# The low parts of the seven operand forms, made by GpSimd in place of VectorE

## The chip, the core and the metric

One core of a Trainium2 chip runs the whole program. A core has five engines that run their own instruction lists and meet at semaphores: TensorE (PE, with its weight loads shown as PEld), VectorE (DVE), ScalarE (ACT), GpSimd (POOL) and SyncE (SP, which here only starts DMAs). The metric is the device time of one execution in microseconds (us). The kernel before was timed three times: 2039.69, 2042.03 and 2042.06, median 2042.03.

## The reference

One decoder layer on 512 tokens of width 2048 in float32: an adaptive modulation, a mixer made of a gated recurrence and an attention with a forget bias, and an MLP with squared ReLU. The change lies in the MLP alone:

```python
def rms_norm(x, g):
    xf = x.astype(jnp.float32)
    y = xf * lax.rsqrt(jnp.mean(jnp.square(xf), axis=-1, keepdims=True) + EPS)
    return (y * g.astype(jnp.float32)).astype(x.dtype)
...
        x = x + gt1[:, None, :] * rms_norm(y, g_post_mix[l])
        h = modulate(rms_norm(x, g_pre_mlp[l]), sh2, sc2)
        y = jnp.square(jax.nn.relu(h @ w_ff1[l])) @ w_ff2[l]
        x = x + gt2[:, None, :] * rms_norm(y, g_post_mlp[l])
```

`w_ff1` is 2048 x 8192 and `w_ff2` is 8192 x 2048.

## The kernel before

**Arithmetic.** Every float32 operand of a matmul is split in two parts of the type fp32r: a high part, which ACT makes by a copy that rounds, and a low part, the float32 value less the high part, which DVE makes. A product takes three matmuls: high by low, low by high, high by high. Both MLP products use a scheme with seven half-size products in place of eight (named P1, P5, P6, P3, P7, P2, P4 in the order of work), whose operands are sums of quadrants.

**The first MLP product (stage A).** The 8192 hidden columns are cut into 32 blocks of 256 (`b`). The first four are made in the usual way. For the other 28, each block is seven units on PE (`first_product`, L1142 to L1144), one for each of the seven products, and a unit is 8 x 3 matmuls of 128x256. For each unit the weight tile, or a sum of quadrants of it that DVE makes (`total`, L2210), is split: `high` on ACT (L1602), `low` on DVE (L2161). Three of the seven results stay in a bank that is read by ACT (`copy_sum`, L1579) and three are added by DVE to what was copied (`add_sum`, L2218). PE may not start P4 of a block until DVE has added P7, since both use one bank; nor P6 until ACT has copied P1.

**Closing a block.** When P4 of a block is done, ACT applies the ReLU (`rectify`, L1552 and L1554) and the square (`square_u`, L1560), which gives four quadrants of `u_forms`. DVE makes four sums of them (`operand_sums`, L2139 to L2144). Slots 1 to 7 of `u_forms` are then the seven forms, 128x1792. ACT copies them rounded to `hi_stage` (`operand_high`, L1573), DVE subtracts in place (`operand_low`, L2150), and GpSimd, whose list in this stage is nothing else, stores both parts to a scratch in HBM (`store_forms`, L2510 and L2512). Each store waits for its own part. The next block's `rectify` and `operand_high` wait until both stores of the block before have landed (`stored_through`), since there is one `u_forms` and one `hi_stage`.

**What sets the order.** The order on each engine is written out by hand. DVE and ACT run one loop over the units: at PE's unit n, DVE makes the low part of unit n + 2, adds or reads the result of unit n - 1, and makes the sum for unit n + 4; ACT makes the high part of unit n + 3. `CLOSE_AT[b]` gives the unit at which a block is closed: `rectify` there, the sums one unit on, `operand_high` two, `operand_low` three. For most blocks that is the first unit of the next block; blocks 4 and 5 are closed one unit later, and the last block (31) three units after stage A has ended.

**The second MLP product (stage B).** SP loads the stored forms into `op`, 1 MB at a time, and the `w_ff2` tiles; PE runs 16 groups of seven products (L1160 to L1162), DVE makes weight sums and low parts and reads the products out of PSUM (`read_product`, L2235 and L2237). P7 of a group may start only when DVE has read P6.

Of the kernel before, what the change touches and what calls it, by code (L numbers as in the profile page):

```python
# [16 lines left out]
F32 = mybir.dt.float32  # L17
F32R = mybir.dt.float32r
ALU = mybir.AluOpType
# [13 lines left out]
def hybrid_layer(nc, x, c, w_ada, b_ada, g_pre_mix, g_post_mix, g_pre_mlp, g_post_mlp, w_in, conv_w, conv_b,  # L33
# [24 lines left out]
    for which, (_, j0, j1) in enumerate(PASSES):  # L58
        for j in range(j0, j1):
            if which:  # L60
                BACK_UNIT[j] = len(FIRST_UNITS)
                FIRST_UNITS.append((which, j - j0))
            P_UNIT[j] = len(FIRST_UNITS)
            FIRST_UNITS.append((which, j))
            Q_UNIT[j] = len(FIRST_UNITS)
            FIRST_UNITS.append((None, j))
    assert len(BACK_UNIT) == 6
    DONE_PAIRS = {gi: j1 for gi, _, j1 in PASSES if gi is not None}
    V_FROM = [DONE_PAIRS.get(gi, 0) for gi in range(8)]
    START = [8 * gi - sum(V_FROM[:gi]) for gi in range(9)]  # L70
# [41 lines left out]
    BLOCKS = D_FF // 256  # L112
    FIRST = 4
    U_A = U_MLP + CONV
# [17 lines left out]
    def a_unit(n):  # L132

        return divmod(n - U_A, 7)
# [14 lines left out]
    def made_of_sums(n):  # L149

        if n >= U_END:
            return False
        if n < U_B:
            return 1 <= a_unit(n)[1] <= 4
        return b_unit(n)[1] in SUM_INDEX
# [44 lines left out]
    with ExitStack() as ctx:  # L200
# [3 lines left out]
        def sem(name):  # L204
            return ctx.enter_context(nc.semaphore(name))

        def overlay(*specs):

            with ExitStack() as phase:
                return [phase.enter_context(nc.sbuf_tensor(n, s, d)) for n, s, d in specs]  # L210
# [27 lines left out]
            ("h_hi", [P, KT, COLS], F32R), ("x_tok", [P, NT, D], F32), ("gst0", [P, 8, 2, 256], F32),  # L238
            ("xnT", [P, KT, COLS], F32), ("gst1", [P, 8, 2, 256], F32), ("junk", [P, D], F32))
        _, h_lo, hs, rg, ig, ut, wrg, wig, a_sq, sq = overlay(  # L240
            ("pad2", [P, KT, COLS], F32), ("h_lo", [P, KT, COLS], F32R), ("hs", [P, CT, COLS], F32),
            ("rg", [P, CT, COLS], F32), ("ig", [P, CT, COLS], F32), ("ut", [P, CT, COLS], F32),
# [16 lines left out]
        _, T34, u_forms, ext, T12, hsO = overlay(  # L259
            ("pad5", [P, 32 * 256], F32), ("T34", [P, 8, 2, 2, 256], F32R), ("u_forms", [P, 8, 256], F32), ("ext", [P, 4 * COLS], F32),  # L260
            ("T12", [P, 8, 2, 2, 256], F32R), ("hsO", [P, 2, 8, 2, 256], F32R))
# [40 lines left out]
        def stage_of(b):  # L302

            if b >= 3:
                return hi_stage[:, :, :]
            place_ = rows_base[:, :, :].rearrange("p a (s n) -> p (a s) n", n=256) if b == 0 else k_tile[2]
            return place_[:, 0:7, :].bitcast(F32R)
# [46 lines left out]
        with ExitStack() as whole:  # L354
# [66 lines left out]
        relu_done, u_done, u_sum, op_hi_ready, op_lo_ready = (  # L421
            sem(n) for n in ("relu_done", "u_done", "u_sum", "op_hi_ready", "op_lo_ready"))
# [1278 lines left out]
        def _(dve):  # L1701
# [433 lines left out]
            def operand_sums(b):  # L2135

                dve.wait_ge(u_done, b + 1)
                F = u_forms
                dve.tensor_tensor(F[:, 4, :], F[:, 0, :], F[:, 2, :], ALU.add).then_inc(u_sum, 1)  # L2139
                dve.tensor_tensor(F[:, 7, :], F[:, 1, :], F[:, 0, :], ALU.subtract).then_inc(u_sum, 1)  # L2140
                dve.wait_ge(u_sum, 4 * b + 1)
                dve.tensor_tensor(F[:, 5, :], F[:, 4, :], F[:, 1, :], ALU.subtract).then_inc(u_sum, 1)
                dve.wait_ge(u_sum, 4 * b + 3)
                dve.tensor_tensor(F[:, 6, :], F[:, 3, :], F[:, 5, :], ALU.subtract).then_inc(u_sum, 1)  # L2144

            def operand_low(b):

                dve.wait_ge(op_hi_ready, b + 1)
                F = u_forms[:, 1:8, :]
                dve.tensor_tensor(F.bitcast(F32R), F, stage_of(b).bitcast(F32), ALU.subtract).then_inc(op_lo_ready, 1)  # L2150

            def low(n):

                if n < U_A:
                    return lo_part(n)
                dve.wait_ge(hi_ready, n + 1)
                if n < U_B:
                    out_, w, hi = by_tile(w_lo, n), a_source(n), by_tile(w_hi, n)
                else:
                    out_, w, hi = w_lo[:, n % RING, :], b_source(n), w_hi[:, n % RING, :]  # L2160
                dve.tensor_tensor(out_, w, hi.bitcast(F32), ALU.subtract).then_inc(lo_ready, 1)  # L2161
# [50 lines left out]
            def add_sum(n):  # L2212

                blk, pos = a_unit(n)
                dve.wait_ge(unit_used, n + 1)
                dve.wait_ge(c_copied, 3 * blk + {P3: 3, P7: 2, P2: 1}[pos])
                s = c_sums[:, blk % 2, {P3: 0, P7: 2, P2: 1}[pos], :]
                dve.tensor_tensor(s, s, a_bank(blk, pos), ALU.add).then_inc(c_added, 1)  # L2218
# [3 lines left out]
            def read_product(m):  # L2222

                g, i = divmod(m, 7)
                kind = KINDS[g][i]
                K, r = divmod(g, 2)
                dve.wait_ge(unit_used, U_B + 2 * m + 2)
                if m:
                    dve.wait_ge(y_read, reads_before(m))
                targets = [(1, 0)] * ((g, kind) == (GROUPS - 1, P7)) + [TARGETS[kind]]  # L2230
                for th, side in targets:
                    y = y2[:, 2 * th:2 * th + 2, y_cols(0, side, r)]
                    bank = pairs_of(g, kind)[:, :, :]
                    if K == 0 and kind in (P1, P5, P6, P4):
                        ins = dve.tensor_copy(y, bank)  # L2235
                    else:
                        ins = dve.tensor_tensor(y, y, bank, ALU.add)  # L2237
                    ins.then_inc(y_read, 1)
# [60 lines left out]
            def gate_first(t):  # L2299
                dve.wait_ge(f_ssq, t + 1)  # L2300
                if t == 0:
                    dve.wait_ge(g2_in, 16)
                y = tile_cols(y2[:, t, :], 0)
                gated_at[t, 0] = gate_piece(y, y, None)

            def gate_inside(t, side, square):
                dve.wait_ge(f_ssq, square)
                cols = y_cols(t, side, 1)
                gated_at[t, 1] = gate_piece(y2[:, t, cols], y2[:, t, cols], cols)

            for n in range(U_A, U_END):
                if n + 2 < U_END:
                    low(n + 2)
                if U_A < n <= U_B and a_unit(n - 1)[1] in (P3, P7, P2):
                    add_sum(n - 1)
                if n > U_B and (n - U_B) % 2 == 0:
                    read_product((n - U_B) // 2 - 1)
                if made_of_sums(n + 4):
                    total(n + 4)
                for b, at in CLOSE_AT.items():  # L2320
                    if n - U_A == at + 1:
                        operand_sums(b)
                    elif n - U_A == at + 3:
                        operand_low(b)
                tail = n - G_LAST
                for t in {3: [0], 4: [1], 5: [2, 3]}.get(tail, []):
                    gate_first(t)
                if tail in (6, 11):
                    for t in range(2):
                        gate_inside(t, 0 if tail == 6 else 1, (5 if tail == 6 else 7) + t)  # L2330
# [46 lines left out]
        def _(pool):  # L2377
# [128 lines left out]
            def store_forms(b):  # L2506

                K, i = divmod(b, 4)
                pool.wait_ge(op_hi_ready, b + 1)
                pool.dma_start(u_scr[K, :, :, 0, i, :], stage_of(b).bitcast(F32)).then_inc(u_stored[b % 2], 16)  # L2510
                pool.wait_ge(op_lo_ready, b + 1)
                pool.dma_start(u_scr[K, :, :, 1, i, :], u_forms[:, 1:8, :]).then_inc(u_stored[b % 2], 16)  # L2512

            for b in range(BLOCKS):
                store_forms(b)
            pool.wait_ge(gate_stored, 16 * 8)
            pool.wait_ge(unit_used, U_B)
# [33 lines left out]
```

## Time and profile before

| | |
|---|---|
| median of three runs | 2042.03 us |
| the profiled execution | 2040.41 us, span 2038.6 us |
| PE busy | 1995.0 us, 98% of the span |
| DVE busy | 1739.0 us, 85% |
| ACT busy | 950.7 us, 47% |
| POOL busy | 141.7 us, 7% |
| granted PE clock | 0.993 of full |

The profiled execution's own time is 1.8 us over its span, for what lies before the first and behind the last instruction. Busy shares are means over the whole program. PE is the engine to look at first, and for the others the question at each place is how long before PE needs it their work is done. Stage A of the 28 blocks runs from about 839 us to 1410 us, stage B from there to the end.

### The profile page before, as it was taken

To read this page: it belongs to the slowest core of one execution; us is meant where nothing else is said; L and a number is where in the kernel's file an instruction comes from. 1 tells how busy PE (TensorE), PEld (TensorE's weight loads), DVE (VectorE), ACT (ScalarE), POOL (GpSimd) and SP (SyncE) were. 2 spreads that over 40 slices of the span, in tenths; PEclk is the share of its full clock that TensorE was granted. 3 is DMA by queue.
4 is the path that set the end of the run, shared out by engine and by line. 5 is a ranking of instruction groups with operands and counts; after the bars stand their busy time and mean duration, and the time that the engine had idled before them with its cause. 6 is when DMAs were issued, how large, how long until landed. Compare 5 with 4: busy or idle time off the path is not lost.

```text
span 2038.6 us, 28073 instructions
## 1 busy us (share of the span) xinstructions
PE 1995.0 (98%) x11091; PEld 1727.8 (85%) x11091; DVE 1739.0 (85%) x2010; ACT 950.7 (47%) x1208; POOL 141.7 (7%) x160
## 2 busy tenths in 40 slices
PE   7999999999999989999999999999999999999996
PEld 5887788888778878899999999999888888888885
DVE  7999897786987888788888888888988888888889
ACT  6434632224553267565656555555333333333343
POOL 2001120001120000100101010100000000000000
PEclk8999999999999999999999999999999999999998
DMA  9986668966438753656565656668956656656642
GB/s 369 392 284 188 215 180 290 296 195 204 137 132 280 272 184 124 217 176 212 188 201 194 199 196 198 198 198 296 345 188 231 212 179 228 215 177 229 218 152 103
DMA packets 233891, 442.99 MB, mean 217 GB/s; under 512 B 12600, under 2 KB 111080, under 8 KB 224288
## 3 DMA queue, kind: packets, MB, share of 16 engines
q1 hardware_dynamic: 210464, 360.79, 53.1%
q0 software_dynamic: 18928, 75.68, 10.3%
q10 hardware_dynamic: 4368, 4.73, 0.7%
q8 instruction: 88, 1.44, 0.3%
q14 instruction: 43, 0.35, 0.1%
HBM read 371.92 MB, written 69.24 MB: 216 GB/s over the span
## 4 chain that ended last, share of the span: by engine, by line
PE 83%; DVE 11%; DMA 2%; ACT 2%; issue 2%; DVEq 0%; SPq 0%; ACTq 0%
PE bank L1142 9%; PE bank L1143 9%; PE bank L1144 9%; PE pair L1160 9%; PE pair L1161 9%; PE pair L1162 9%; PE bank L677 6%; PE bank L679 5%; PE bank L678 5%; PE bank L689 3%; PE bank L691 3%; PE bank L690 3%; DVE rows_base L1746 1%; DVE w_lo L1714 1%; DVE w_lo L2161 1%
## 5 line engine op out<-in xcount | busy, mean ns | idle before, releaser
L1160 PE MATMUL pair<-w_hi,op 128*128 128x512 f32 x896 | 349.3, 390 | 0.8 <-DVE y L2235 0.5
L1161 PE MATMUL pair<-w_lo,op 128*128 128x512 f32 x896 | 348.6, 389 | 0.0
L1162 PE MATMUL pair<-w_hi,op 128*128 128x512 f32 x896 | 348.6, 389 | 0.0
L1218 ACT ACTIVATE w_hi<-raw 128x1024 fp32r<-128x1024 f32 (+1 forms) x130 | 134.9, 1045 | 276.3 <-DMA raw<-in_w_in_dram 159.9
L1142 PE MATMUL bank<-T,w_lo 128*128 128x256 f32 x896 | 254.5, 284 | 4.6 <-ACT c_sums L1579 4.6
L1143 PE MATMUL bank<-T,w_hi 128*128 128x256 f32 x896 | 254.2, 284 | 0.0
L1144 PE MATMUL bank<-T,w_hi 128*128 128x256 f32 x896 | 254.2, 284 | 0.0
L1602 ACT ACTIVATE w_hi<-w_tiles 128x1024 fp32r<-128x1024 f32 x128 | 135.9, 1062 | 218.0 <-PE pair L1162 184.2
L1746 DVE SCALAR_TENSOR_TENSOR rows_base<-raw,cc,rows_base 128x512 f32<-128x512 f32 x224 | 178.2, 796 | 29.8 <-DMA raw<-in_w_ada_dram 19.6
L1714 DVE TENSOR_TENSOR w_lo<-raw,w_hi 128x1024 fp32r<-128x1024 f32 (+1 forms) x129 | 162.3, 1260 | 45.1 <-ACT w_hi L1218 43.5
L1160 PEld LDWEIGHTS pair<-w_hi,op 128*128 128x128 f32 x896 | 168.2, 188 | 37.0 <-DVE y L2235 0.9
L1162 PEld LDWEIGHTS pair<-w_hi,op 128*128 128x128 f32 x896 | 168.2, 188 | 35.1
L1161 PEld LDWEIGHTS pair<-w_lo,op 128*128 128x128 f32 x896 | 168.2, 188 | 34.9 <-issue 0.2
L677 PE MATMUL bank<-h_hi,w_lo 128*128 128x512 f32 x496 | 197.4, 398 | 0.4
L679 PE MATMUL bank<-h_hi,w_hi 128*128 128x512 f32 x496 | 193.2, 390 | 0.0
L678 PE MATMUL bank<-h_lo,w_hi 128*128 128x512 f32 x496 | 193.0, 389 | 0.0
L1602 ACT ACTIVATE w_hi<-rows_base 128x1024 fp32r<-128x1024 f32 x112 | 119.0, 1062 | 149.6 <-PE bank L1144 139.7
L2161 DVE TENSOR_TENSOR w_lo<-raw,w_hi 128x1024 fp32r<-128x1024 f32 x121 | 147.8, 1222 | 47.7 <-ACT w_hi L1602 47.7
L1602 ACT ACTIVATE w_hi<-raw 128x1024 fp32r<-128x1024 f32 x121 | 127.9, 1058 | 123.0 <-PE pair L1162 97.3
L1142 PEld LDWEIGHTS bank<-T,w_lo 128*128 128x128 f32 x896 | 172.8, 193 | 4.9 <-issue 4.9
L1143 PEld LDWEIGHTS bank<-T,w_hi 128*128 128x128 f32 x896 | 172.7, 193 | 0.0
L1144 PEld LDWEIGHTS bank<-T,w_hi 128*128 128x128 f32 x896 | 172.7, 193 | 0.0
(350 smaller groups left out, 4334.0 us busy)
## 6 DMA issues: line engine op xcount, KB each, us to landing
raw<-in_w_ff_dram SPq DMA_DIRECT2D x70, 1024.0 KB, 6.1
raw<-in_w_ada_dram SPq DMA_DIRECT2D x128, 512.0 KB, 4.7
op<-u_scratch SPq DMA_DIRECT2D x56, 1024.0 KB, 6.8
raw<-in_w_in_dram SPq DMA_DIRECT2D x74, 512.0 KB, 4.8
ext<-in_w_ff_dram SPq DMA_DIRECT2D x34, 1024.0 KB, 6.9
gst<-in_w_ada_dram SPq DMA_DIRECT2D x64, 512.0 KB, 8.1
u_scratch<-u_forms POOLq DMA_DIRECT2D x32, 896.0 KB, 6.9
u_scratch<-hi_stage POOLq DMA_DIRECT2D x29, 896.0 KB, 4.4
```

The source lines that it names most:

```text
L677: pe.matmul(b[:, :], lo[:, cols], act_hi[:, kt, :], start=(kt == first), stop=False)
L678: pe.matmul(b[:, :], hi[:, cols], act_lo[:, kt, :], start=False, stop=False)
L679: last = pe.matmul(b[:, :], hi[:, cols], act_hi[:, kt, :], start=False, stop=(kt == n_kt - 1))
L1142: pe.matmul(out_, lo, moving(pos, j, 0), start=(fresh and j == 0), stop=False, skip_group_check=True)
L1143: pe.matmul(out_, hi, moving(pos, j, 1), start=False, stop=False, skip_group_check=True)
L1144: last = pe.matmul(out_, hi, moving(pos, j, 0), start=False, stop=(j == 7), skip_group_check=True)
L1160: pe.matmul(bank[:, tt, :], op_lo, hi, start=(start and fresh and h == 0 and k == 0), stop=False, skip_group_check=True)
L1161: pe.matmul(bank[:, tt, :], op_hi, lo, start=False, stop=False, skip_group_check=True)
L1162: last = pe.matmul(bank[:, tt, :], op_hi, hi, start=False, stop=(h == 1 and k == 1), skip_group_check=True)
L1602: act.activation(dst, w, ACT.Copy).then_inc(hi_ready, 1)
L1714: dve.tensor_tensor(w_lo[:, s, cells], raw[:, slot, cells], w_hi[:, s, cells].bitcast(F32), ALU.subtract).then_inc(lo_ready, 1)
L1746: ins = dve.scalar_tensor_tensor(a, row, cc[:, 2, k:k + 1], a if k else acc_init[:, :], ALU.mult, ALU.add)
```

## The change

DVE no longer makes the low part of the forms for blocks 3 to 31. GpSimd makes it, in its own list, with the same instruction on the same operands: it waits for the high part, subtracts, and then issues both stores. Blocks 0 to 2 are as before. `operand_low` stays in the code for those three.

```diff
@@ the loop of DVE over the units @@
                 for b, at in CLOSE_AT.items():
                     if n - U_A == at + 1:
                         operand_sums(b)
-                    elif n - U_A == at + 3:
-                        operand_low(b)
@@ the list of GpSimd @@
-            for b in range(BLOCKS):
+            for b in range(3):
+                store_forms(b)
+            for b in range(3, BLOCKS):
+                pool.wait_ge(op_hi_ready, b + 1)
+                F = u_forms[:, 1:8, :]
+                pool.tensor_tensor(F.bitcast(F32R), F, stage_of(b).bitcast(F32), ALU.subtract).then_inc(op_lo_ready, 1)
                 store_forms(b)
```

On DVE, at the place in a block where its high part has been made. The names: `w_lo` and `w_hi` are the split weight tiles, `raw`, `ext` and `rows_base` hold weight tiles and their sums, `c_sums` the partial results.

```order
 L2144 TENSOR_TENSOR u_forms<-u_forms 128x256
 L2161 TENSOR_TENSOR w_lo<-rows_base,w_hi 128x1024
-L2161 TENSOR_TENSOR w_lo<-raw,w_hi 128x1024
-L2150 TENSOR_TENSOR u_forms<-u_forms,hi_stage 128x1792
-L2161 TENSOR_TENSOR w_lo<-raw,w_hi 128x1024
+L2161 TENSOR_TENSOR w_lo<-raw,w_hi 128x1024 x2
 L2218 TENSOR_TENSOR c_sums<-c_sums,bank 128x256
 L2210 TENSOR_TENSOR rows_base<-raw,ext 128x1024
```

One instruction is gone from DVE's list, and its neighbours stand next to each other; nothing else moved.

On GpSimd, the two stores of block 2 and those of blocks 3 and 4 before the change (line numbers of the kernel before):

```order
L2510 DMA u_scratch<-ext 896x1x256
L2512 DMA u_scratch<-u_forms 896x1x256
L2510 DMA u_scratch<-hi_stage 896x1x256
L2512 DMA u_scratch<-u_forms 896x1x256
L2510 DMA u_scratch<-hi_stage 896x1x256
L2512 DMA u_scratch<-u_forms 896x1x256
```

The same place in the changed kernel (its own line numbers, two lower for the stores):

```order
L2508 DMA u_scratch<-ext 896x1x256
L2510 DMA u_scratch<-u_forms 896x1x256
L2517 TENSOR_TENSOR u_forms<-u_forms,hi_stage 128x1792
L2508 DMA u_scratch<-hi_stage 896x1x256
L2510 DMA u_scratch<-u_forms 896x1x256
L2517 TENSOR_TENSOR u_forms<-u_forms,hi_stage 128x1792
L2508 DMA u_scratch<-hi_stage 896x1x256
L2510 DMA u_scratch<-u_forms 896x1x256
```

The subtraction stands ahead of both stores, so the store of the high part, which before was issued as soon as that part was made, is now issued behind it.

## Rows read from the trace of the kernel before

**Rows 1.** Stretches: length, busy us of each engine (instructions), granted clock, DMA share, GB/s.

```profile
1000.00:1200.00 200.00, 200.00 (x1669) 200.00 (x1668) 172.49 (x189) 117.73 (x139) 17.91 (x20) 1.00 0.60 195
```

**Rows 2.** DVE in order of time, block 16: start, length, engine, line [idle before].

```profile
1116.96 2.03 DVE L2150 TENSOR_TENSOR u_forms<-u_forms,hi_stage 128x1792 fp32r<-128x1792 f32 x1 [0.37 <-ACT hi_stage L1573]
1118.90 1.22 DVE L2161 TENSOR_TENSOR w_lo<-raw,w_hi 128x1024 fp32r<-128x1024 f32 x1
1120.04 0.42 DVE L2218 TENSOR_TENSOR c_sums<-c_sums,bank 128x256 f32<-128x256 f32 x1
...
1122.65 0.42 DVE L2218 TENSOR_TENSOR c_sums<-c_sums,bank 128x256 f32<-128x256 f32 x1
```

**Rows 3.** ACT and PE in order of time, block 16.

```profile
1115.23 1.69 ACT L1573 ACTIVATE hi_stage<-u_forms 128x1792 fp32r<-128x1792 f32 x1
...
1117.17 1.06 ACT L1602 ACTIVATE w_hi<-raw 128x1024 fp32r<-128x1024 f32 x1
...
1125.32 0.28 PE L1142 MATMUL bank<-T,w_lo 128*128 128x256 f32 x1
```

**Rows 4.** POOL and DVE at the same time, in the mixer at 288 us.

```profile
288.25 1.33 POOL L2410 TENSOR_TENSOR ssq<-ssq,ut 128x512 f32<-128x512 f32 x1 [2.19 <-ACT ut L1317]
288.34 2.33 DVE L1714 TENSOR_TENSOR w_lo<-raw,w_hi 128x1024 fp32r<-128x1024 f32 x1
```

**Rows 5.** One line's durations, min/median/max in ns: POOL elementwise work.

```profile
L2427 POOL TENSOR_TENSOR nFm<-nF,causal x8: 1272/1286/2197, 466.2 to 585.5; 128x512 f32<-128x512 f32 x8
L2385 POOL MEMSET rows_base<- x1: 518/518/518, 1.7 to 1.7; 128x512 f32 x1
L2414 POOL MEMSET wf<- x1: 1809/1809/1809, 340.7 to 340.7; 128x2048 f32 x1
L2410 POOL TENSOR_TENSOR ssq<-ssq,ut x6: 1328/1564/2098, 282.8 to 293.7; 128x512 f32<-128x512 f32 x6
```

**Rows 6.** DVE, ACT and PE in order of time, block 4.

```profile
877.61 0.42 DVE L2218 TENSOR_TENSOR c_sums<-c_sums,bank 128x256 f32<-128x256 f32 x1 [0.29 <-PE bank L1144]
877.95 1.22 DVE L2210 TENSOR_TENSOR rows_base<-raw,ext 128x1024 f32<-128x1024 f32 x1
...
882.16 0.41 DVE L2218 TENSOR_TENSOR c_sums<-c_sums,bank 128x256 f32<-128x256 f32 x1
...
875.96 1.69 ACT L1573 ACTIVATE hi_stage<-u_forms 128x1792 fp32r<-128x1792 f32 x1
...
883.17 0.28 PE L1142 MATMUL bank<-T,w_lo 128*128 128x256 f32 x1
```

**Rows 7.** POOL in order of time, the two stores of block 16.

```profile
1117.22 0.94 POOL L2510 DMA_DIRECT2D u_scratch<-hi_stage  x1 [17.17 <-ACT hi_stage L1573]
1119.76 0.93 POOL L2512 DMA_DIRECT2D u_scratch<-u_forms  x1 [1.60 <-DVE u_forms L2150]
```

**Rows 8.** Landing times of L2510, then L2512, over all blocks (from each line's page).

```profile
DMA to landing us min/median/max: 4.4/4.5/11.3
DMA to landing us min/median/max: 4.4/6.9/13.7
```

**Rows 9.** What L1552 waited for; then ACT in order of time.

```profile
  DMA u_scratch<-u_forms: 3.1, 3
1114.01 0.38 ACT L1579 ACTIVATE c_sums<-bank 128x256 f32<-128x256 f32 x1 [1.18 <-PE bank L1144]
...
1130.10 0.39 ACT L1552 ACTIVATE u_forms<-bank 128x256 f32<-128x256 f32 x1 [0.57 <-DMA u_scratch<-u_forms]
...
1132.37 0.37 ACT L1579 ACTIVATE c_sums<-bank 128x256 f32<-128x256 f32 x1
```

**Rows 10.** DVE, ACT and PE in order of time, block 31 at stage B's start.

```profile
1426.43 1.22 DVE L2210 TENSOR_TENSOR w_tiles<-raw,w_tiles 128x1024 f32<-128x1024 f32 x1
1427.57 1.22 DVE L2161 TENSOR_TENSOR w_lo<-w_tiles,w_hi 128x1024 fp32r<-128x1024 f32 x1
1428.70 1.22 DVE L2235 COPY y<-pair 128x1024 f32<-128x1024 f32 x1
1429.83 2.02 DVE L2150 TENSOR_TENSOR u_forms<-u_forms,hi_stage 128x1792 fp32r<-128x1792 f32 x1
...
1425.41 1.71 ACT L1573 ACTIVATE hi_stage<-u_forms 128x1792 fp32r<-128x1792 f32 x1
...
1432.23 0.39 PE L1160 MATMUL pair<-w_hi,op 128*128 128x512 f32 x1
```

## The prediction

> **What bounds the kernel now.** I read the table of stretches first. Of the 200 us between 1000 and 1200, PE is busy 200.00 and DVE 172.49 [rows 1]. Its 1669 matmuls there are 0.12 us apart, so a unit of 24 takes 2.88 us and a block of seven units 20.16 us. PE stands still for nothing in stage A, and work taken off DVE can't make it faster: the 28 blocks cost 28 x 20.16 us whatever DVE does. The question is only what is late enough to make PE wait. So I then read DVE, ACT and PE in order of time around one block's closing, and looked for the distance between each piece of work and the matmul that needs it.
>
> Call x the end of `operand_high`, 1115.23 + 1.69 = 1116.92 in block 16 [rows 3]. There DVE starts the low part at x + 0.04 and takes 2.03 us; then comes the low weight part of unit P4, and at x + 5.73 the addition of P7, done at 1123.07, x + 6.15 [rows 2]. P4's first matmul, which needs that addition, is at 1125.32, x + 8.40 [rows 3]. DVE is 2.25 us early. In block 4, which is closed a unit later, x is 877.65, the addition ends at 882.57 and P4 starts at 883.17, x + 5.52: only 0.60 us early [rows 6]. Block 5 has the same pattern.
>
> **What the change removes.** 29 instructions of 2.03 us, 59 us of DVE [rows 2]. At no place in stage A does PE wait for DVE, so this is worth nothing by itself there; it can only buy distance.
>
> **What it adds: GpSimd's subtraction.** The trace has no POOL instruction of 1792 elements. The nearest has two SBUF inputs and 512 elements: 1.286 us undisturbed [rows 5]. If nothing of it were fixed cost, 1792 would take 1.286 x 3.5 = 4.5 us. If the fixed part were as much as 0.35 us, it would be 3.6. The two memsets say how large it is: 0.518 us for 512 and 1.809 for 2048 give 0.84 ns an element and 0.09 fixed [rows 5]. With 0.1 fixed the subtraction takes 0.1 + 3.5 x 1.19 = 4.25. I take 4.1, between that and the lower end, and keep 3.6 to 4.5. The Trainium skill (GPSIMD Engine Reference, Performance versus the Vector engine) gives 4497 ns for this operation at 2048 elements; with the trace's 1.286 at 512 an estimate by it is 3.96 us. No run so far shows it.
>
> **What it adds: DVE stands still meanwhile.** In the mixer POOL reads SBUF from 288.25 to 289.58. DVE's subtraction with two SBUF inputs, usually 1.22 us in this shape [rows 2], starts at 288.34 and takes 2.33, to 290.67: 1.09 us, nearly its whole usual length, behind POOL's end [rows 4]. And POOL's own line, undisturbed at 1.33, has a median of 1.564 over the six [rows 5]. So the two don't share, they take turns by whole instructions. That agrees with the Trainium skill (SBUF — State Buffer, Who interferes with whom): a DVE instruction with two SBUF inputs and a GpSimd instruction that reads SBUF exclude one another until the first is done. If instead they shared by elements, DVE would keep about half its speed; that is the third case below.
>
> Regular blocks (3 and 6 to 30). POOL starts at about x + 0.1 and ends at x + 4.2. DVE's low part for P4 can't start before ACT's high part, at 1118.23, x + 1.31 [rows 3], so POOL always comes first; DVE finishes it at x + 4.2 + 1.09 = x + 5.3 in place of 1120.12, x + 3.2. From the end of that to the end of P7's addition are 1123.07 - 1120.12 = 2.95 us [rows 2]: x + 8.25, against P4 at x + 8.40. So the spare 2.25 us are used up to the last 0.15. PE doesn't wait, if POOL takes 4.1. At 4.25 the cost is still about 0; at 4.5 it is 0.25 us or a little more in each of some 22 blocks, 6 us; at 3.6 it is nothing. I take 1 us for all of them, since a few blocks have a little less distance.
>
> Blocks 4 and 5. At x + 0.1 DVE is in an addition with one input in PSUM, and POOL gets in before the weight sum at 877.95 [rows 6]. That sum ends at x + 4.2 + 1.09, the low part behind it 1.14 later (1120.04 - 1118.90 [rows 2]), and P7's addition 0.42 behind that: x + 6.85, against P4 at x + 5.52. PE waits 1.3 us in each: 2.6 us. With POOL at 3.6 it is 0.8 each, at 4.5 1.7.
>
> **What it moves: the stores.** The high part's store was issued at x + 0.30 and the low part's at x + 2.84 (most often x + 2.35, one issue and the wait for DVE less) [rows 7]. Both are now issued behind the subtraction, at x + 4.2 and x + 5.15. Before, the low part landed 6.9 us after its issue by the median [rows 8], so 8.9 us after the high part's issue. If the pair keeps that it lands at x + 13.1, and if it loses the 1.1 us between the issues, at x + 12.0; I take x + 12.6. The next `rectify` would start at 1130.10 - 0.57 - 1116.92 = x + 12.6 at the latest undelayed point [rows 9]. So ACT waits nothing to 0.5 us, and its 1.18 us of idle time two units later [rows 9] takes that up before the next `operand_high`.
>
> Slow landings. In three blocks `rectify` waited for the store already before, 3.1 us in all [rows 9]. In these the low part landed some 3.4 us later than the median (block 16's before 1130.10, 10.3 us behind its issue). If it is so again, ACT is 3.5 us late. Its copy of P1 ends 2.64 us after `rectify` starts (1132.37 + 0.37 - 1130.10) [rows 9], so at x + 12.5 + 3.5 + 2.64 = x + 18.65. P6 starts at 1125.32 + 3 x 2.88 = 1133.96, x + 17.04. PE waits 1.6, and 0.6 more when the late high part brings POOL closer to P4: 2.2. Two such blocks in the steady stretch cost 4.5 us; none costs 0, four cost 9.
>
> Start of stage B. Block 31's x is 1427.12. POOL comes in when DVE's weight sum has ended, 1427.65, and ends at 1431.7 [rows 10]. DVE's low part behind that ends at 1432.75 and the copy of P6 out of PSUM at 1433.9 in place of 1429.92; PE's P7, which needs it, would start at 1432.23 [rows 10]. PE waits 1.6 us. The 2.02 us that DVE no longer spends at 1429.83 come too late for that. Between -0.5 (if the later loads gain what PE lost) and 2.
>
> **The sum.** 1.0 + 2.6 + 4.5 + 1.6 = 9.7 us. The profiled execution goes from 2040.4 to 2050.1. It was 1.6 us below the median of the runs, so the median goes to 2051.7; I say 2051.5.
>
> **The rivals.** *The block's chain becomes longer than 20.16 us.* The chain is `rectify` to x, 7.65 us with 1.18 of idle time in it, so 6.47; POOL and the two issues 5.15; the landing L. With L = 7.5 it is 19.1 and fits. If the low part's own landing, now queued behind a high part that has hardly begun, takes 10 us, it is 21.6 and PE loses 1.4 us in each of some 22 blocks: 31 us, 2073 to 2080. Halfway to it (L = 9, or POOL at 4.5) lie 6 to 15 us more than my sum: 2058 to 2066. For it: the spread of landings up to 13.7 [rows 8]. Against: three of four blocks land at the median, and POOL's packets have nothing else in their queue.
>
> *No change.* DVE and POOL share by elements: then DVE gets through about 2 us of its work while POOL runs, reaches P7's addition before x + 8, blocks 4 and 5 lose 0.3 each, and if slow landings don't come back either, the time is 2041 to 2045. For it: only that 512 elements is all the trace shows. Against: rows 4 fit taking turns to 0.1 us.
>
> *Faster, the other side.* Stage B's start is the one place where DVE stands on the chain: its low weight part at 1431.77, right behind the removed subtraction [rows 10], releases a load. If POOL doesn't hold DVE there (it decides from a hold of under 2 us), that load goes out 2 us sooner and PE saves up to 2; with nothing lost in stage A, 2040. More than that the profile has no room for.
>
> *The change doesn't do what it says.* Not possible here by the order: DVE's list has 29 subtractions less and POOL's 29 more.
>
> **How the numbers follow.** Forecast as worked out, 2045 to 2057: 0.57. Chain too long, or POOL so slow that every block waits: 0.22. No change: 0.17. Faster: 0.04. What a measurement of this kernel tells from no change is about 0.2%, 4 us. Slower by more is the forecast and the first rival, 0.79; the same 0.17; faster by more than that 0.04 at most. The range from 2043.5 to 2067 holds the forecast, half of the no-change case and two thirds of the first rival. The likeliest case's own range is 2045 to 2057.
>
> **What would show it.** Right: POOL's subtraction at 3.9 to 4.3 us; DVE's w_lo instruction behind `operand_high` lasting about 4 us in place of 1.22; P7's addition ending within 0.3 us of P4's first matmul; PE idle 1.3 us ahead of P4 in blocks 4 and 5 and about 1.6 at 1432; ACT waiting for the store at L1552 in more blocks than three. Wrong: a w_lo instruction there of 1.22 us (no turns), PE idle at P4 in every block (POOL too slow or the chain too long), or a DMA wait at L1552 that grows from block to block.

## The result, and the profile after

The changed kernel takes 2113.65 us by the median of four runs (2113.17 to 2114.49), the kernel before beside it 2041.03 (four runs). The ratio is 1.0357, with a 95% interval from 1.0339 to 1.0375: 73 us slower. The forecast was 2051.5 us, 10 us slower, with a range up to 2067. The direction was right, and the loss was more than seven times the forecast one. The profiled execution has a span of 2111.6 us against 2038.6.

The stretch from 1000 to 1200 us, which answers to [rows 1] (length, busy us of each engine with its instructions, granted clock, DMA share, GB/s):

```profile
1000.00:1200.00 200.00, 181.64 (x1463) 179.04 (x1462) 152.60 (x155) 104.14 (x124) 51.74 (x26) 0.98 0.55 171
```

PE, without a gap before, is idle for 18 of the 200 us and gets through 1463 matmuls in place of 1669. The growth is in stage A. One group of its matmuls, those of `T` by the low weight part, begins and ends with it; here are the starts of its first and last one (with duration min/median/max in ns ahead), before and then after:

```profile
L1142 PE MATMUL bank<-T,w_lo x896: 283/283/553, 842.3 to 1410.1; 128*128 128x256 f32 x180
```

```profile
L1142 PE MATMUL bank<-T,w_lo x896: 278/283/551, 843.1 to 1482.0; 128*128 128x256 f32 x180
```

That is 567.8 and 638.9 us, 71.1 more. The rest of the span has grown by 73.0 - 71.1 = 1.9 us, 1.6 of them at the start of stage B, below. What PE and ACT waited for from 840 to 1482 us (engine, line, releaser: us in all, times, longest):

```profile
ACT u_forms L1552 <- DMA u_scratch<-u_forms: 78.2, 24, 4.3
...
PE bank L1142 <- ACT c_sums L1579: 50.0, 25, 5.0
...
PE bank L1142 <- DVE c_sums L2218: 5.1, 17, 1.2
```

PE stands ahead of P6, waiting for ACT's copy of P1, and ACT is late because the ReLU that closes the block waited for the stores of the block before. DVE itself, ahead of P4, is good for only 5 us.

The landing of the low part's store over all blocks, as the second line of [rows 8]:

```profile
DMA to landing us min/median/max: 4.4/11.5/12.6
```

11.5 us by the median in place of 6.9. Block 16 in the changed kernel, first GpSimd and SP's DMA queue, then DVE, the rows that answer to [rows 2] and [rows 7]; x, the end of `operand_high`, is 1149.77 here:

```profile
1149.85 4.08 POOL L2517 TENSOR_TENSOR u_forms<-u_forms,hi_stage 128x1792 fp32r<-128x1792 f32 x1 [17.08 <-ACT hi_stage L1573]
1153.86 0.95 POOL L2508 DMA_DIRECT2D u_scratch<-hi_stage  x1
1154.71 1.08 POOL L2510 DMA_DIRECT2D u_scratch<-u_forms  x1
...
1155.04 0.37 SPq L512 DMA_DIRECT2D raw<-in_w_ff_dram  x1
...
1151.02 3.99 DVE L2161 TENSOR_TENSOR w_lo<-raw,w_hi 128x1024 fp32r<-128x1024 f32 x1 [1.42 <-ACT w_hi L1602]
1154.93 0.41 DVE L2218 TENSOR_TENSOR c_sums<-c_sums,bank 128x256 f32<-128x256 f32 x1
...
1157.54 0.41 DVE L2218 TENSOR_TENSOR c_sums<-c_sums,bank 128x256 f32<-128x256 f32 x1
```

GpSimd subtracts for 4.08 us. DVE's low part of P4 lasts 3.99 us in place of 1.22 and ends 1.08 us behind it. Its end releases a 1 MB load of `w_ff1` on SP's queue, which is issued 0.33 us behind the low part's store (0.41 us in most blocks). What happened then, in the same block (ACT and PE, as [rows 9]):

```profile
1166.74 0.38 ACT L1552 ACTIVATE u_forms<-bank 128x256 f32<-128x256 f32 x1 [3.96 <-DMA u_scratch<-u_forms]
...
1168.99 0.37 ACT L1579 ACTIVATE c_sums<-bank 128x256 f32<-128x256 f32 x1
...
1169.50 0.36 PE L1142 MATMUL bank<-T,w_lo 128*128 128x256 f32 x1 [2.55 <-ACT c_sums L1579]
```

The low part landed at 1166.66, 11.95 us after its issue. ACT had waited 3.96 us for it, and PE 2.55 us for the copy. The DMA queues between 1158.7 and 1160.9 us, when both stores and the load had long been issued (queue 0 has GpSimd's stores, queue 1 SP's loads; packets, MB, share of 16 engines):

```profile
q1 hardware_dynamic: 489, 0.50, 84.3%
q0 software_dynamic: 10, 0.00, 0.2%
```

and in the kernel before, block 17, between 1141.6 and 1144.6, with its low part's store and the same load under way:

```profile
q0 software_dynamic: 193, 0.79, 87.1%
q1 hardware_dynamic: 139, 0.14, 14.4%
```

Before, the store has the engines almost to itself and the load gets the rest. After, the load has them and the store stands still, although it was issued first.

The waits of PE in the table above don't add up to 71 us. One of the 25 for ACT, of 5.0 us at 851 us, was there before as well (4.6), so some 50 us are new; counted from start to start of the matmuls, the new gaps are 57 us. Most of the rest is PE at a lower clock: in eight stretches of 3.4 us, each beginning within 1.5 us of the end of a wait ahead of P6, the granted clock is 0.50, which is 1.2 GHz. PE's matmuls are 0.21 us apart there in place of 0.12, so it starts 16 in place of 28 and loses 1.5 us in each stretch, 12 us in all. This is no second cause. From the landing of the low part to the next x (the end of the next block's `operand_high`) it is 6.45 or 6.46 us in every block from 6 to 29, with such a stretch or without: the chain of stores sets the block's length, and the slow stretch takes up time that PE would have waited (in block 11, behind one, the gap ahead of P6 is 1.04 us where the neighbours have 2.1 and 3.0).

### The profile page after: what moved, and what is told of

Same layout as the page of the kernel before. It is cut to its first block, busy times and chain, and to the rows that moved or that the text cites. A ratio compares the mean times of both kernels' runs of the same rounds, so it can differ in the third digit from the quotient of the medians.

```text
span 2111.6 us, 28073 instructions
## 1 busy us (share of the span) xinstructions
PE 2014.7 (95%) x11091; PEld 1740.9 (82%) x11091; DVE 1748.3 (83%) x1981; ACT 949.6 (45%) x1208; POOL 259.6 (12%) x189
## 3 DMA queue, kind: packets, MB, share of 16 engines
q0 software_dynamic: 18928, 75.68, 10.3%
## 4 chain that ended last, share of the span: by engine, by line
PE 64%; DVE 11%; DMA 10%; ACT 7%; POOL 4%; issue 3%; DVEq 0%; ACTq 0%
DMA u_scratch<-u_forms 10%; PE pair L1160 9%; PE pair L1162 9%; PE pair L1161 9%; PE bank L677 5%; PE bank L679 5%; PE bank L678 5%; PE bank L1142 3%; POOL u_forms L2517 3%; PE bank L1144 3%; PE bank L1143 3%; PE bank L689 3%; PE bank L690 3%; PE bank L691 3%; ACT w_hi L1602 2%
## 5 line engine op out<-in xcount | busy, mean ns | idle before, releaser
L1142 PE MATMUL bank<-T,w_lo 128*128 128x256 f32 x896 | 262.7, 293 | 55.1 <-ACT c_sums L1579 50.0
L1143 PE MATMUL bank<-T,w_hi 128*128 128x256 f32 x896 | 259.5, 290 | 0.0
L1144 PE MATMUL bank<-T,w_hi 128*128 128x256 f32 x896 | 259.3, 289 | 0.0
L2161 DVE TENSOR_TENSOR w_lo<-raw,w_hi 128x1024 fp32r<-128x1024 f32 x121 | 190.7, 1576 | 65.1 <-ACT w_hi L1602 65.1
L1142 PEld LDWEIGHTS bank<-T,w_lo 128*128 128x128 f32 x896 | 177.8, 198 | 62.4 <-issue 59.7
L2517 POOL TENSOR_TENSOR u_forms<-u_forms,hi_stage 128x1792 fp32r<-128x1792 f32 x29 | 118.2, 4076 | 487.9 <-ACT hi_stage L1573 487.9
L1144 PEld LDWEIGHTS bank<-T,w_hi 128*128 128x128 f32 x896 | 178.0, 199 | 0.0
## 6 DMA issues: line engine op xcount, KB each, us to landing
u_scratch<-u_forms POOLq DMA_DIRECT2D x32, 896.0 KB, 11.5
```

Of the source, the lines that this page charges most:

```text
L1142: pe.matmul(out_, lo, moving(pos, j, 0), start=(fresh and j == 0), stop=False, skip_group_check=True)
L1143: pe.matmul(out_, hi, moving(pos, j, 1), start=False, stop=False, skip_group_check=True)
L1144: last = pe.matmul(out_, hi, moving(pos, j, 0), start=False, stop=(j == 7), skip_group_check=True)
L2517: pool.tensor_tensor(F.bitcast(F32R), F, stage_of(b).bitcast(F32), ALU.subtract).then_inc(op_lo_ready, 1)
```

## The experiments

Two theories were to be told apart. Theory 1: the load overtakes the low part's store, because both are released by the end of GpSimd's subtraction and the load's packets are on the engines first. Theory 2: the stores are late, or slow, for another reason: the lateness of the subtraction, or simply 0.9, 0.9 and 1 MB at the same time. In what follows the distance is the time from the issue of the low part's store to the issue of the load, and the landing is counted from the store's issue; both are for blocks 6 to 29, read from the issues and landings in each trace.

**The load later by some 5 us.**

```diff
-                    sp.wait_ge(lo_ready, U_A + 7 * (blk - 1))
+                    sp.wait_ge(lo_ready, U_A + 7 * (blk - 1) + 2)
```

> The changed kernel, with one wait of the DMA queue moved: the load of each block's even w_ff1 tile waits for two more low parts on DVE (those of P1 and P5), so that it is issued some 5 us later than now. Theory 1 (the load overtakes the store): in the changed kernel the end of GpSimd's subtraction releases both the low part's store (x + 4.84) and, by way of DVE's held low part, this load (x + 5.26), and the load's packets run ahead of the store's, so that the store lands 11.7 us after its issue. Without the load beside it, as in blocks 4 and 5 of the changed kernel, it lands after 6.1 us, the block's chain is 6.5 + 4.9 + 6.1 = 17.5 us and fits into 20.16, and the time falls to 2047 us (2044 to 2052): what is left is 1.35 us in each of blocks 4 and 5, under 1 us in block 6 and 1.6 at stage B's start. Theory 2 (the stores are late because the subtraction is late, whatever else is on the queue): 2100 to 2115, landings stay at 11 to 12 us.

2044.9 us (ratio 1.0020, 1.0011 to 1.0030). The landing of L2510:

```profile
DMA to landing us min/median/max: 4.3/6.2/10.4
```

PE is busy 200.00 of 200 us again, with GpSimd's subtraction and the hold on DVE in every block as in the changed kernel:

```profile
1000.00:1200.00 200.00, 200.00 (x1669) 200.00 (x1669) 178.08 (x180) 116.98 (x139) 59.03 (x30) 1.00 0.59 198
```

69 of the 73 us were in the meeting of load and store. Two stores back to back, with nothing beside them, land quickly; my rival's reason, a store queued behind another, is not it. The 10.4 in the line is block 29: its load is the first one of `w_ff2`, whose wait this edit doesn't move, so there the distance stayed at 0.42 us, and PE waited 0.96 us ahead of the next P6. In one execution, the same two stores took 6.2 us with the load moved and 10.4 without.

**The high part's store ahead of the subtraction.**

```diff
                 pool.wait_ge(op_hi_ready, b + 1)
+                pool.dma_start(u_scr[K, :, :, 0, i, :], stage_of(b).bitcast(F32)).then_inc(u_stored[b % 2], 16)
                 F = u_forms[:, 1:8, :]
...
-                store_forms(b)
+                pool.wait_ge(op_lo_ready, b + 1)
+                pool.dma_start(u_scr[K, :, :, 1, i, :], u_forms[:, 1:8, :]).then_inc(u_stored[b % 2], 16)
```

> The changed kernel, with the high part's store issued ahead of the subtraction, as before the change. The store takes GpSimd 0.94 us, so the subtraction runs from about x + 1.25 to x + 5.3. Theory 1 (overtaking decides by the distance between store and load): DVE's low part of P4 ends at x + 6.4, the load follows at x + 6.5, 1.1 us behind the low part's store at x + 5.35, which is more than the 0.87 us that the store had before the change; it lands after about 7 us and the chain fits. But P7's addition now ends at x + 9.3 against P4 at x + 8.4, so PE waits 1.0 us at P4 in every block: 2063 to 2075 us. Theory 2 (lateness alone): landings of 11 to 12 us and PE waiting for the copy of P1: over 2110.

2079.5 us (1.0188, 1.0172 to 1.0203), 4.5 us over the expectation. The landing fell to 6.2 us at a distance of 0.82 us, as theory 1 has it; in blocks 8, 16 and 24, where the distance was 0.10 to 0.34, it took 9.0 to 10.0. The other expected loss is there in its place. Block 17, where x is 1156.81, GpSimd, DVE and PE:

```profile
1157.88 4.28 POOL L2519 TENSOR_TENSOR u_forms<-u_forms,hi_stage 128x1792 fp32r<-128x1792 f32 x1
...
1158.05 5.20 DVE L2161 TENSOR_TENSOR w_lo<-ext,w_hi 128x1024 fp32r<-128x1024 f32 x1 [1.42 <-ACT w_hi L1602]
...
1165.77 0.41 DVE L2218 TENSOR_TENSOR c_sums<-c_sums,bank 128x256 f32<-128x256 f32 x1
...
1166.33 0.36 PE L1142 MATMUL bank<-T,w_lo 128*128 128x256 f32 x1 [1.23 <-DVE c_sums L2218]
```

The hold on DVE begins a microsecond later, and the 0.2 us that were left ahead of P4 become a wait: 0.95 us in most blocks, 1.23 in this one. A block takes 21.34 us in place of 20.16, 1.2 more, where I had put 1.0. At the start of stage B the gap ahead of P7 is 2.7 us too.

**DVE makes the low part, and both stores stand behind it.** (The kernel before, one wait added.)

```diff
             for b in range(BLOCKS):
+                if b >= 3:
+                    pool.wait_ge(op_lo_ready, b + 1)
                 store_forms(b)
```

> The kernel before, with DVE still making the low part; alone the high part's store is moved behind it. No GpSimd arithmetic, no hold on DVE. High part's store at x + 2.35, low part's at x + 3.1, the load at x + 3.22, 0.1 us behind. Theory 1 (overtaking): the low part lands 11 to 12 us after its issue, at x + 14.8, the chain is 6.5 + 14.9 = 21.4 us, and PE loses 1.2 us in each of some 24 blocks: 2065 to 2075 us, though no engine does more work. If GpSimd's hold on DVE were needed for the loss: 2041, as before.

2065.9 us (1.0125, 1.0108 to 1.0142). The landing of the low part's store over all blocks:

```profile
DMA to landing us min/median/max: 4.4/11.4/12.2
```

No engine does more work than before, and DVE is not held. What the change does to the two queues is enough for 25 us. In the changed kernel the same slow store is issued 1.76 us later (x + 4.85 against x + 3.09), and 24 times 1.76 is 42 us more, which is most of what is missing to 73.

**GpSimd as long busy, but without reading.** (The low parts are not computed, zeros are stored.)

```diff
-                pool.tensor_tensor(F.bitcast(F32R), F, stage_of(b).bitcast(F32), ALU.subtract).then_inc(op_lo_ready, 1)
+                pool.memset(F, 0.0).then_inc(pool_step, 1)
+                pool.wait_ge(pool_step, 4 + 2 * (b - 3))
+                pool.memset(F, 0.0).then_inc(pool_step, 1)
+                pool.wait_ge(pool_step, 5 + 2 * (b - 3))
+                pool.memset(u_forms[:, 1:4, :], 0.0).then_inc(op_lo_ready, 1)
```

> The changed kernel, with three memsets (1792, 1792 and 768 elements, about 4.1 us in all) on GpSimd in place of the subtraction: GpSimd is busy as long and the stores are issued as late, but it reads no SBUF; the low parts are not computed (they are stored as zeros). If the hold comes from GpSimd's reads, DVE's low part of P4 takes 1.22 us again and ends at x + 2.5, and the load is issued at x + 2.6, 1.5 us ahead of the stores. Theory 1: the load is out of the way by about x + 7.5, both stores then run at full rate and the low part lands at about x + 12.8, so ACT waits 0.3 us: 2041 to 2045 us. Theory 2 (lateness of the stores alone): 2100 or more. If memsets hold DVE as well, DVE's low part lasts about 4 us and the time stays near 2113.

2044.9 us (1.0020, 1.0010 to 1.0030). DVE's low part of P4 in block 18, while GpSimd is at its memsets:

```profile
1160.88 1.23 DVE L2161 TENSOR_TENSOR w_lo<-raw,w_hi 128x1024 fp32r<-128x1024 f32 x1 [1.50 <-ACT w_hi L1602]
```

1.23 us: memsets don't hold DVE, so the hold comes from GpSimd's reads. The stores are issued as late as in the changed kernel (the low part's at x + 4.8), but the load goes 1.6 us ahead of the first, and 69 us are gone. Lateness alone is refuted. (A store that comes this far behind the load took 9.05 us by the median, less than one that comes just ahead of it.) The low part landed at x + 13.3 to 15.1 in most blocks, not at 12.8; ACT waited in 24 blocks, 38.6 us in all, and PE lost about 5.

**The distance alone.** Three kernels like the one before, with one, two and three memsets on GpSimd ahead of the low part's store.

```diff
                 pool.wait_ge(op_lo_ready, b + 1)
+                if b >= 3:
+                    pool.wait_ge(pool_step, b)
+                    pool.memset(ssq[:, :], 0.0).then_inc(pool_step, 1)
                 pool.dma_start(u_scr[K, :, :, 1, i, :], u_forms[:, 1:8, :]).then_inc(u_stored[b % 2], 16)
```

> The kernel before, with one memset of 512 elements (0.52 us) on GpSimd ahead of each low part's store from block 3 on. DVE, the high part's store, the bytes and the load are as before; the low part's store alone is issued at about x + 2.87 in place of x + 2.35, and the load stays at x + 3.22. Theory 1 (the distance between store and load decides which of them goes first): the distance falls from 0.87 to 0.35 us, as it was by chance in block 16 of the kernel before, and the landing rises from 6.9 us to 10 us or more in nearly every block; it lands at x + 13 to 13.5, ACT waits some 0.5 to 1 us in most blocks and makes it good, so the time stays at 2040 to 2046 us. Theory 2 (the bytes that are on their way at the same time set the landing): 6.4 to 7.5 us, since they are the same.

2040.3 us (1.0000, 0.9991 to 1.0009). The expectation was missed: the landing stayed at 6.5 us. But the edit did less than it should. Half of the memset's time was time in which the store had waited anyway, and the store moved by 0.24 us, to a distance of 0.64. In block 8, where GpSimd was slower to issue, the distance was 0.50 and the landing 10.5 us. So the next two had one memset of 128 elements more, and two:

```diff
                     pool.wait_ge(pool_step, b)
+                    pool.memset(vrow[:, :], 0.0)
                     pool.memset(ssq[:, :], 0.0).then_inc(pool_step, 1)
```

> The kernel before, with two memsets on GpSimd (128 and 512 elements) ahead of each low part's store. With one memset the store had moved by only 0.24 us, to 0.63 us ahead of the load, and landed as before; in block 8 alone, where the distance was 0.50, it took 10.5 us. One more memset (about 0.2 us) makes the distance some 0.44 us. Theory 1 (the distance decides, and the turn lies between 0.63 and 0.50): the low part's store takes 9 to 11 us in nearly every block, at the same bytes, with DVE and the high part's store untouched; it lands at x + 12.5 to 13.5, which ACT's idle time covers: 2039 to 2044 us. Theory 2 (bytes on their way): 6.1 to 7.5 us as with one memset, and block 8 was chance.

```diff
                     pool.wait_ge(pool_step, b)
+                    pool.memset(vrow[:, :], 0.0)
+                    pool.memset(causal[:, :], 0.0)
                     pool.memset(ssq[:, :], 0.0).then_inc(pool_step, 1)
```

> The same with three memsets (128, 128 and 512 elements), distance about 0.24 us. Theory 1: 10 to 12 us in nearly every block, landing at x + 13 to 14.5; ACT waits 0.5 to 2 us in most blocks, PE up to 0.3 us in each: 2040 to 2048 us. Theory 2: 6.1 to 7.5 us, 2040 to 2042.

The landing with one, two and three memsets, over all blocks:

```profile
DMA to landing us min/median/max: 4.4/6.5/13.1
```

```profile
DMA to landing us min/median/max: 4.4/8.9/13.2
```

```profile
DMA to landing us min/median/max: 4.4/8.8/13.2
```

The distances were 0.64, 0.49 and 0.34 us. In blocks 6 to 29 the landings were 6.5, 9.4 and 8.9 us by the median, and none of the two last kernels was under 8.3. A store 0.15 us later takes 2.9 us longer, and another 0.15 us adds nothing. So the landing doesn't grow with the nearness of the load; there is a turn, a distance below which the load goes first, and the bytes are the same on both sides of it. The times were 2040.35 (0.9995, 0.9984 to 1.0005) and 2040.25 us (0.9992, 0.9983 to 1.0002), no difference, since these blocks had 3 us to spare.

**Can the distance alone save the changed kernel?** The load waits for one, and then for two more instructions of DVE.

```diff
                     sp.wait_ge(lo_ready, U_A + 7 * (blk - 1))
+                    sp.wait_ge(c_added, 3 * (blk - 2) + 1)
```

> The changed kernel; the load of each block's even w_ff1 tile waits in addition for the next instruction in DVE's list, the addition of P3, which ends 0.42 us behind the low part that releases it now. So the load is issued at about x + 5.7, 0.84 us behind the low part's store in place of 0.42, and overlaps it in full: the bytes on their way are the same to 0.4 us. Theory 1 (the turn lies between 0.63 and 0.50 us of distance): the store keeps ahead, lands 7.5 to 8.5 us after its issue in place of 11.7, at x + 12.4 to 13.3, the chain of 6.5 + 4.9 + 8 = 19.4 us fits into 20.16, and the time falls from 2113 to 2044 to 2050 us, as with the load 5 us later. Theory 2 (three transfers of 0.9, 0.9 and 1 MB at the same time need that long): the landing stays at 11 to 12 us and the time at 2105 to 2115.

2108.0 us (1.0340, 1.0312 to 1.0367). Theory 1 as I had put it was wrong here: at a distance of 0.78 us the store was still overtaken, with a median landing of 11.7 us in blocks 6 to 29. Over all blocks:

```profile
DMA to landing us min/median/max: 4.4/11.3/13.0
```

Only in blocks 26 and 27, at 0.81 and 0.82, did it take 7.8 and 8.1. So the turn is not at one distance for all kernels. Where the high part's store is 2.3 us ahead it lies between 0.49 and 0.64. Where both stores are issued back to back it lies above 0.78, and near 0.80 if these two blocks of one trace are typical.

```diff
                     sp.wait_ge(lo_ready, U_A + 7 * (blk - 1))
+                    sp.wait_ge(w_sum, 4 * (blk - 1) + 1)
```

> The changed kernel; the load of the even tile waits for the weight sum that DVE makes behind the addition of P3, so it is issued at about x + 6.8, 1.95 us behind the low part's store (0.42 in the changed kernel, 0.79 with one wait less). With 0.79 the store was still overtaken in 21 of 24 blocks, landing after 11 to 13 us, but in blocks 26 and 27, at 0.81 and 0.82, it took 7.8 and 8.1. Theory 1 in its mended form (the store goes ahead if its packets are there before the load's, and a store issued right behind another has them later, so that the turn lies at 0.80 here and at 0.5 to 0.63 where the high part's store is 2.3 us ahead): 6.5 to 8.3 us in nearly every block, landing at x + 11.5 to 13.1, and 2043 to 2050 us. Theory 2 (the bytes on their way): the load still overlaps the stores for all but 1.2 us more than in the last run, so the landing is 10 us or more and the time 2085 us or more.

2047.95 us (1.0035, 1.0022 to 1.0047), the landing over all blocks:

```profile
DMA to landing us min/median/max: 4.4/7.9/12.3
```

At a distance of 1.92 us, with the load still beside the stores, 65 of the 73 us are gone. Theory 2 had 2085 or more. Of the 3 us that this kernel takes longer than the one with the later load, 1.6 are in block 4, where another load came 0.46 us behind the store, the store took 12.3 us, and PE waited ahead of P6.

**The subtraction in two halves.** (With the later load of the first experiment.)

```diff
-                F = u_forms[:, 1:8, :]
-                pool.tensor_tensor(F.bitcast(F32R), F, stage_of(b).bitcast(F32), ALU.subtract).then_inc(op_lo_ready, 1)
+                for a, z in ((0, 4), (4, 7)):
+                    F, H = u_forms[:, 1 + a:1 + z, :], stage_of(b)[:, a:z, :]
+                    ins = pool.tensor_tensor(F.bitcast(F32R), F, H.bitcast(F32), ALU.subtract)
+                ins.then_inc(op_lo_ready, 1)
```

> The changed kernel with the later load, and GpSimd's subtraction in two instructions, of 1024 and 768 elements. If the two engines take turns by whole instructions, DVE gets its turn between them: its low part for P4, which waits from x + 1.31, ends at about x + 3.6 (a duration of 2.3 us in place of about 4), GpSimd's second half ends at about x + 5.3 in place of x + 4.2, and the sum that DVE makes after that lasts about 2.4 us in place of 1.22. If they shared by elements, two halves would look like one: the low part for P4 ends at x + 5.2 as before. The time: 2044 to 2048 us either way.

2044.2 us (1.0018, 1.0008 to 1.0028). GpSimd starts its two at 1141.12 and ends the second at 1146.31; DVE in the same time:

```profile
1142.36 2.24 DVE L2161 TENSOR_TENSOR w_lo<-ext,w_hi 128x1024 fp32r<-128x1024 f32 x1 [1.66 <-ACT w_hi L1602]
1144.52 0.41 DVE L2218 TENSOR_TENSOR c_sums<-c_sums,bank 128x256 f32<-128x256 f32 x1
1144.85 2.54 DVE L2210 TENSOR_TENSOR rows_base<-raw 128x1024 f32<-128x1024 f32 x1
```

Two holds of 1.0 and 1.3 us in place of one of 2.8, as for two engines that take turns by whole instructions. The addition between them, which has one input in PSUM, lasts its usual 0.41.

**What is left, and whether the relief is worth anything.** The low part of blocks 3, 4, 5 and 31 goes back to DVE, with the later load.

```diff
+                    elif n - U_A == at + 3 and not 6 <= b <= 30:
+                        operand_low(b)
...
+                if not 6 <= b <= 30:
+                    store_forms(b)
+                    continue
```

> The changed kernel with the later load, and the low part of blocks 3, 4, 5 and 31 made by DVE again, so that GpSimd makes it for blocks 6 to 30 alone. If what is left of the loss in the kernel with the later load (4.2 us) is the wait ahead of P4 in blocks 4 and 5 (2 x 1.3 us) and the one at stage B's start (1.4 us), this kernel is within 1 us of the kernel before: 2040 to 2042 us, and not below it, since PE stood still for DVE nowhere in stage A. If the 51 us of work taken off DVE are worth anything, it is faster than the kernel before by more than 1 us.

2040.44 us against 2040.36 (1.0000, 0.9991 to 1.0009). The trace has none of the waits ahead of P4 and at stage B's start any more; what it still has is block 29's meeting of store and load (distance 0.41 us, PE's wait 0.98 us), which is too small to be told from no change in these times. 25 subtractions fewer on DVE bring nothing that shows: this is the best that any version with GpSimd's subtraction reached, and it only equals the kernel before.

## Why the prediction was wrong

**What failed.** One step: "If the pair keeps that it lands at x + 13.1, and if it loses the 1.1 us between the issues, at x + 12.0; I take x + 12.6." It landed at x + 16.5 by the median, 4.85 + 11.7; the issue at 4.85 was even 0.3 us earlier than forecast, and the landing time of 11.7 is what was wrong. The step carried a landing over from a trace in which the load came 0.87 us behind the store, to a kernel in which it comes 0.41 behind. I had worked out both issue times: the store's stands in the prediction, and the load's follows from the held low part, x + 5.3. I never set them side by side. They fall together by construction, since GpSimd's end starts its own stores and frees DVE, which frees the load.

**The price.** Put the measured landing into the chain of the prediction's first rival: 6.5 + 4.85 + 11.7 = 23.05 us a block, 2.9 over 20.16. Over 24 blocks that waited for a store it is 70 us; stage A grew by 71. Term by term, the sum had 1.0 us for regular blocks held too long (measured: nothing by itself), 2.6 for blocks 4 and 5 (2.6), 1.6 for stage B's start (1.6), and 4.5 for late landings, which is the term that became some 68. The rival had the form right, a chain longer than PE's period, and was given 0.22. Its reason was wrong (without the load two stores back to back take 6.2 us), and so was its bound of 10 us for the landing, under the 13.7 of [rows 8].

**The sign that was there.** "Slow landings" were taken as chance and priced at 4.5 us. (The landing 3.4 us later than the median is that of blocks 8 and 16; the third block in which `rectify` waited is block 5, with 7.7 us.) Block 16 had its store at 1119.76 [rows 7] and lay at a distance of 0.39 us from its load, blocks 8 and 24 at 0.15 and 0.39; the landings were 10.3, 10.2 and 8.7 us. All other blocks from 6 to 29 lay at 0.85 to 0.87 and took 6.4 to 7.5. A table of distances against landings, from the trace of before, would have shown that near loads and slow landings go together. The prediction's own list of signs could not have found the error: everything that it names under "right" was there in the changed kernel, ACT's waits "in more blocks than three" too, with a time 62 us off.

**What held.** GpSimd's subtraction: 4.1 us forecast, 4.07 by the median. DVE's hold: P7's addition was to end at x + 8.25 and ended at x + 8.17. Regular blocks lose nothing to it by itself, as the first experiment shows. Blocks 4 and 5: 1.3 us each forecast; here are DVE's weight sum and PE's P4 in block 4, where x is 878.72, as [rows 6]:

```profile
879.02 4.93 DVE L2210 TENSOR_TENSOR rows_base<-raw,ext 128x1024 f32<-128x1024 f32 x1
...
885.56 0.35 PE L1142 MATMUL bank<-T,w_lo 128*128 128x256 f32 x1 [1.16 <-DVE c_sums L2218]
```

P4 starts at x + 6.84 where it stood at x + 5.52: 1.32 us. The start of stage B: 1.6 us forecast, P7's wait for the copy of P6 as [rows 10]:

```profile
1505.80 0.50 PE L1160 MATMUL pair<-w_hi,op 128*128 128x512 f32 x1 [1.45 <-DVE y L2235]
```

The gap to the matmul before is 1.83 us where 0.23 is usual, so 1.6. These terms are 4.2 us of the 9.7. The kernel with the later load loses as much, 2044.9 against 2040.7, but that the two are equal to a tenth is in part luck: its trace has block 29's wait on top, 1.1 us that no term foresaw.

**The other cases.** No change needed engines that share by elements; the two halves refute it. Faster needed a hold of under 2 us at stage B's start, which lasted 3.9.

**Open.** Why a store issued before a load can be overtaken. The packets in the traces show a part of it. With nothing ahead of it in its queue, the first packet of GpSimd's store comes 1.52 us after the start of its issue (the high part's, blocks 6 to 29 of the kernel before), and that of SP's load 1.03 to 1.06 us after its own (nearly all of those in the kernel with the later load). So a store that is issued less than about 0.49 us ahead of the load has its first packet behind the load's, and the turn was measured between 0.49 and 0.64. That the turn moves to about 0.80 behind another store would fit packets that come later still, but no run shows when a second store's packets could have started. Nor does any show why the load, once first, keeps the store from moving at all. Nor did a run take apart why the landing is 11.7 us in the changed kernel and 9.4 where only the low part's store is overtaken.

## What to carry to other kernels

When a change makes one event release two transfers, write both issue times under each other: here 0.15 us in the distance between them was worth 3 us of landing, and 1.5 us in the start of a load was worth 65 us of the kernel. Before work is taken off an engine, look for a place where the bounding engine waits for it; where there is none the relief is worth nothing, and only what the new owner delays counts. A hold on a neighbour engine is priced by what stands next behind it: the same 4 us cost nothing in 24 blocks with 2.25 us of distance and a little idle time, and 1.3 us in each of two blocks with 0.6.

## What the runs showed of the hardware

- GpSimd's subtraction of two SBUF tensors of 128x1792 takes 4.07 us, DVE's 2.03. With [rows 5] that is 2.2 ns an element.
- While it runs, a DVE instruction with two SBUF inputs doesn't proceed; it ends 1.08 us behind GpSimd's end (128x1024). An addition with one input in PSUM lasts its usual 0.41 us, and memsets on GpSimd leave DVE at 1.23. This agrees with the Trainium skill (SBUF — State Buffer, Who interferes with whom).
- A DMA from GpSimd's queue can be passed by one that SP issues later. The turn lay between 0.49 and 0.64 us of distance, and behind another store of 0.9 MB above 0.78, near 0.80 by two blocks of one trace. The first packet came 1.52 us after the start of GpSimd's issue and 1.03 us after that of SP's, with nothing ahead in the queue. On the wrong side the store moved 10 packets in 2.2 us while the load moved 489; on the right side the store had 85% of the bytes.
- Behind waits of PE the granted clock was 0.50, or 1.2 GHz, for 3.4 us at a time. The matmuls of 128x256 were 0.21 us apart in it, and 0.12 at full clock.
